# Second mixer: the four value and gate chunks projected block by block between the levels of the decayed scores

## The chip, the cores and the metric

The kernel runs on one core of a Trainium2 chip. The metric is the device time of one launch in microseconds, the median of several runs. The time before is 2326.71 us (three runs, 2320.91 to 2326.8).

## The reference, cut to what matters

A sequence of 256 tokens of width 1024 goes through two blocks. The first block has two layers, each a mixer and a mixture of 32 experts; the second has two layers with two feed-forward parts and a mixer each. The change is in the mixer of the first block's second layer, which joins a small attention (MLA) and a gated linear attention (GLA):

```
cq, ckv, krope, gq, gk, gv, gg, lr_f, lr_b = _split(x @ w_in, ODD_SPLITS)
...
k = jnp.concatenate([k_nope, jnp.broadcast_to(k_rope, ...)], -1)
mla = _merge(_blocked_attention(q, k, v, (MLA_NOPE + MLA_ROPE) ** -0.5))
...
o = _bidirectional_scan(gq_h, _heads(gk, GLA_HEADS), _heads(gv, GLA_HEADS), log_gate(lr_f, ...), log_gate(lr_b, ...))
gla = _merge(_rms_norm(o, gla_norm)) * jax.nn.silu(gg)
return jnp.concatenate([mla, gla], axis=-1) @ w_out
```

The values `gv` and the gates `gg` are 512 columns each of `x @ w_in`. The scan needs `gv` only when its scores are multiplied into values, at its very end, and `gg` after that. Nothing in `mla` needs either.

## The kernel before, in words

**Chunks.** `x @ w_in` is computed in eight chunks of 256 columns, `od(0)` to `od(7)`: 4 and 5 are `gv`, 6 and 7 are `gg`. Each weight chunk is loaded as 1 MB into one of seven ring slots (SyncE's queue). ScalarE (ACT) writes its rounded high part (`split_act`, L432, two instructions a chunk), VectorE (DVE) the rest (`split_dve`, L439, two instructions), and only then is the ring slot free for the next load. PE forms high x high + high x low + low x high (`three`), 48 matmuls of 128x256 a chunk, 24 for each of the two token blocks (`project_block_pe`, the matmuls are issued in `mm`, L228). ACT copies the bank out (`evacuate_act`, L564). There are four pairs of part buffers, so the split of chunk 6 waits until PE has used chunk 4, and so on.

**The order.** Each engine has its own queue, in program order, and waits on semaphores. `OD_ORDER` is the order of the attention for all engines, written out by hand: "scores" (PE scores; DVE maximum L771; ACT exponential L781), "gates" (the logarithms of the GLA decay: PE product, DVE L2162 and L1890, ACT Exp L1896 and Ln L1898), "probs" (DVE), "turn" (PE transposes L791), "values", "logs" (DVE L2168), "mix" (ACT copies the result). Heads 0 and 2 go first, then 1 and 3. Before the change chunk 4 is projected ahead of this order, chunks 5 and 6 inside it ("project"), and chunk 7 behind it, where the first chunk of the output weights is split too.

**The decayed scores.** `decayed_pe`, `decayed_act` and `decayed_dve` then form the scores of the scan in both directions (two streams) by halving: level 8, 7, ... 1. In a level PE multiplies `decayed` blocks (L1663 for level 8, L1673 for the others, with 64 rows of the array a head; each fp32 matmul is two records in the trace, so a stream's level is 16 records and a round of both streams 32). For each stream DVE multiplies the factors in (L1740), copies the level above through a mask (L1763, 128x256) and forms the next distance (L1724); ACT takes its exponential (L1731). DVE starts with two running sums (L1682). These functions call `aside(step)` at step 0 and once a round (steps 2 to 9); in this mixer it did nothing. The mixers of the second block use the same functions, with 128 rows a head and half as many records, and there projections do stand in `aside`.

**After it.** `decayed_values_pe` multiplies the scores by `gv` (L228, 128x128), ACT takes squares (L749), DVE and POOL the norm, the gate is multiplied in, and the output is projected (`gated_pe`, `out_pe`). The split of the output chunks releases the ring for the second experts' weights.

Of the kernel before, what the change touches and what calls it, by code (L numbers as in the profile page):

```python
# [524 lines left out]
def project_pe(e, k, key, group=A_BANKS, fresh=None):  # L525


    S = k.S
    bank = k.banks.open(e, group, key)
    if feature_major(key):  # L530
        for c in range(2):
            _, hi, lo = split_views(k, key + (c,))
            e.wait_ge(*S.low[key + (c,)])
            if fresh is not None and c == 0:
                x_ready(e, k, fresh, 1)
            mm(e, bank[:, c * T:(c + 1) * T], three([((hi[:, j, :], lo[:, j, :]), (k.xh[:, j, :], k.xl[:, j, :])) for j in range(KT)])
               ).then_inc(*S.used.tell(key + (c,)))
        return
    for tb in range(NB):
        project_block_pe(e, k, key, bank, tb, fresh)  # L540
# [1352 lines left out]
def log_sigmoid_act(e, k, tmp, key):  # L1893
# [7 lines left out]

OD_ORDER = (("scores", 0), ("scores", 2), ("project", 5), ("gates", 0), ("probs", 0), ("probs", 2), ("project", 6), ("logs", 0),
            ("turn", 0), ("turn", 2), ("gates", 1), ("values", 0), ("values", 2), ("logs", 1),
            ("scores", 1), ("scores", 3), ("probs", 1), ("probs", 3), ("turn", 1), ("turn", 3), ("values", 1), ("values", 3), ("mix", 0), ("mix", 1))
ROPES = slice(MLA_NOPE, MLA_QD)


def od(c):  # L1910
    return "od_in", 0, c
# [42 lines left out]
def od_pe(e, k, n):  # L1954
    S, b = k.S, k.od
    cos, sin, swap = (k.tab(name)[ROPES, :] for name in ("mla_cos", "mla_sin", "mla_swap"))
    project_pe(e, k, od(0), fresh=n)
    project_pe(e, k, od(1))
    project_pe(e, k, od(2), B_BANKS)
    project_pe(e, k, od(3), B_BANKS)  # L1960
    bank = k.banks.open(e, A_BANKS, ("narrow",))
    e.wait_ge(*S.dve_out[od(1)])
    for tb in range(NB):
        ins = e.transpose(bank[:, block(tb)], b.narrow[:, tb, :], k.ident)
    ins.then_inc(*S.product.tell(("narrow",)))
    view = pairs(k.banks.open(e, A_BANKS, ("cqT",))[:, :])
    e.wait_ge(*S.dve_out[od(0)])
    for j in range(2):
        for tb in range(NB):
            ins = e.transpose(view[:, j, block(tb)], b.cq[:, tb, block(j)], k.ident)  # L1970
    ins.then_inc(*S.product.tell(("cqT",)))
    bank = k.banks.open(e, A_BANKS, ("ckvT",))
    e.wait_ge(*S.dve_step["ckv"])
    for tb in range(NB):
        ins = e.transpose(bank[:, block(tb)], b.ckv[:, tb, :], k.ident)
    ins.then_inc(*S.product.tell(("ckvT",)))
    e.wait_ge(*S.wide_loaded["od"])
    for pair in range(2):
        heads = (2 * pair, 2 * pair + 1)
        bank = k.banks.open(e, A_BANKS, ("q_raw", pair))  # L1980
        e.wait_ge(*S.dve_out[("cqT",)])
        for i, h in enumerate(heads):
            ins = mm(e, bank[0:MLA_QD, i * T:(i + 1) * T], [(k.w_uq[:, j, h * MLA_QD:(h + 1) * MLA_QD], b.cqT[:, j, :]) for j in range(2)])
        ins.then_inc(*S.product.tell(("q_raw", pair)))
        bank = k.banks.open(e, A_BANKS, ("k_raw", pair))
        e.wait_ge(*S.dve_out[("ckvT",)])
        for i, h in enumerate(heads):
            ins = mm(e, bank[0:MLA_NOPE, i * T:(i + 1) * T], [(k.w_ukv[:, h * 192:h * 192 + MLA_NOPE], b.ckvT[:, 0, :])])
        ins.then_inc(*S.product.tell(("k_raw", pair)))
        bank = k.banks.open(e, A_BANKS, ("mla_v", pair))  # L1990
        for tb in range(NB):
            for i, h in enumerate(heads):
                ins = mm(e, bank[:, block(tb * 2 + i)], [(b.ckvT[:, 0, block(tb)], k.w_ukv[:, h * 192 + MLA_NOPE:(h + 1) * 192])])
        ins.then_inc(*S.product.tell(("mla_v", pair)))
    bank = k.banks.open(e, A_BANKS, ("k_rope",))
    e.wait_ge(*S.dve_out[("narrow",)])
    mm(e, bank[ROPES, 0:T], [(swap, b.narrow_T[ROPES, 0, :])]).then_inc(*S.product.tell(("k_rope",)))
    for pair in range(2):
        view = pairs(k.banks.open(e, B_BANKS, ("q_rope", pair))[ROPES, :])
        e.wait_ge(*S.act_out["q_raw", pair])  # L2000
        for i in range(2):
            ins = mm(e, view[:, i, :], [(swap, b.qh[ROPES, 2 * pair + i, :])])
        ins.then_inc(*S.product.tell(("q_rope", pair)))
    project_pe(e, k, od(4))
    out_banks = [k.banks.open(e, O_BANKS, ("mla_o", pair)) for pair in range(2)]
    for what, i in OD_ORDER:
        if what == "project":
            project_pe(e, k, od(i))
        elif what == "scores":
            view = pairs(k.banks.open(e, B_BANKS, ("mla", i))[:, :])  # L2010
            e.wait_ge(*S.dve_step["q_roped", i // 2])
            e.wait_ge(*S.act_out["k_raw", 1])
            for tb in range(NB):
                ins = mm(e, view[:, tb, :], [(b.qh[0:MLA_QD, i, block(tb)], b.kh[0:MLA_QD, i, :])])
            ins.then_inc(*S.product.tell(("mla", i)))
        elif what == "turn":
            turn_probabilities_pe(e, k, b.e1[i // 2], ("mla_pt", i), ("mla_p", i))
        elif what == "values":
            e.wait_ge(*S.act_out["mla_pt", i])
            out = out_banks[i // 2][:, (i % 2) * T:(i % 2 + 1) * T]  # L2020
            mm(e, out, [(b.v[:, kb, block(i)], b.pt[i // 2][:, kb, :]) for kb in range(NB)]).then_inc(*S.product.tell(("mla_o", i)))
        elif what == "gates":
            view = pairs(k.banks.open(e, A_BANKS, ("gate_log", i))[:, :])
            rank = slice(32 * i, 32 * i + GATE_RANK)
            for j in range(2):
                ins = mm(e, view[:, j, :], [(k.gla_w2[rank, block(j)], b.narrow_T[rank, 0, :])])
            ins.then_inc(*S.product.tell(("gate_log", i)))
    project_pe(e, k, od(7))
    decayed_pe(e, k, b.streams, lambda step: None)
    decayed_values_pe(e, k, ("gla_o",), b.streams, b.crosses, lambda side, i: 2 * i + side, b.gla_v, od(5))  # L2030
    gated_pe(e, k, "od_out", 0, ("gla_o",), ("mla_mix",))

# [7 lines left out]
def od_act(e, k):  # L2040
    S, b = k.S, k.od
# [11 lines left out]
    for pair in range(2):  # L2053
        for key, tile, r in (("q_raw", b.qh, slice(0, MLA_QD)), ("k_raw", b.kh, slice(0, MLA_NOPE))):
            e.wait_ge(*S.product[key, pair])
            evacuate_act(e, k, (key, pair), tile[r, 2 * pair:2 * pair + 2, :], pairs(k.banks[key, pair][r, :]))
    od_project_act(e, k, 4, b.gla_v[:, :, 0:256])
    for what, i in OD_ORDER:
        if what == "project":
            od_project_act(e, k, i, b.gla_v[:, :, 256:512] if i == 5 else b.gate[:, :, 0:256])  # L2060
        elif what == "scores":
            if i % 2:
                e.wait_ge(*S.product["mla_pt", i - 1])
            softmax_act(e, k, ("mla", i), b.e1[i // 2], MLA_QD ** -0.5, k.tags[:, i // 2, :])
        elif what == "turn":
            if i % 2:
                e.wait_ge(*S.product["mla_o", i - 1])
            e.wait_ge(*S.product["mla_pt", i])
            evacuate_act(e, k, ("mla_pt", i), b.pt[i // 2])
        elif what == "gates":  # L2070
            log_sigmoid_act(e, k, b.la[i], ("gate", i))
        elif what == "mix":
            if i == 0:
                e.wait_ge(*S.masks_made["all"])
            e.wait_ge(*S.product["mla_o", 2 * i + 1])
            evacuate_act(e, k, ("mla_o", i), k.mixT[:, 2 * i:2 * i + 2, :])
    od_project_act(e, k, 7, b.gate[:, :, 256:512])
    decayed_act(e, k, b.streams, lambda step: None)
    e.wait_ge(*S.act_out[od(7)])
    e.activation(b.gate, b.gate, ACT.Silu).then_inc(*S.act_out.tell(("gla_o", "gate")))  # L2080
    e.wait_ge(*S.act_out["mla_o", 1])
# [5 lines left out]
def od_dve(e, k, norm):  # L2087
# [53 lines left out]
    split_chunk(e, k, following(k, od(4)), split_dve)  # L2141
    for what, i in OD_ORDER:
        tags = k.tags[:, (i // 2) % 2, :]
        if what == "project":
            split_chunk(e, k, following(k, od(i)), split_dve)
        elif what == "scores":
            softmax_dve(e, k, ("mla", i), MLA_QD ** -0.5, tags)
        elif what == "probs":
            e.wait_ge(*S.act_out["mla", i])
# [21 lines left out]
    for i in (1, 3):  # L2171
        e.wait_ge(*S.product["mla_o", i])
    e.memset(b.diag.rearrange("p a b c -> p (a b c)"), 0.0).then_inc(*S.dve_step.tell("gla_clear"))
    split_chunk(e, k, following(k, od(7)), split_dve)
    e.wait_ge(*S.dve_step["la", 1])
    e.wait_ge(*S.act_out[od(3)])
    decayed_dve(e, k, b.streams, lambda step: None)
    mix_parts_dve(e, k, k.mixT[:, 0:4, :], (slice(0, P), slice(0, 4), slice(0, T)), ("mla_mix",))
    gated_dve(e, k, "od_out", 0, ("gla_o",), k.gla_norm[:, :], b.gate, ("gla_o", "gate"), norm)

# [765 lines left out]
```

## Time and profile before

| | |
|---|---|
| median of three runs | 2326.71 us |
| span of the profiled execution | 2323.1 us |
| what the runs' median has above that span | 3.6 us |
| TensorE (PE) busy | 2166.1 us, 93% |
| VectorE (DVE) busy | 1142.2 us, 49% |
| ScalarE (ACT) busy | 784.0 us, 34% |
| mean granted TensorE clock | 0.975 |
| HBM traffic over the span | 267 GB/s |

The profiled execution has no run time of its own beside its span, so a change in the span is taken as the same change in the median. Times in a timeline are microseconds from the start of the span. A timeline row says when a merged group of one line starts and how long it lasts; "idle before" is how long its engine had stood still and what ended that. Clock 1.00 is 2.4 GHz, 0.50 is 1.2 GHz.

### The profile page before, as it was taken

The page shows a single profiled execution, that of the slowest core. Times are in us where ns is not written, and L with a number is a line of the kernel's source. Part 1 is how long each engine was busy: PE and PEld are TensorE (multiplying, and loading weights), DVE is VectorE, ACT ScalarE, POOL GpSimd, SP SyncE. Part 2 cuts the span into 40 slices and gives each one's busy share as a digit, 9 for nine tenths or more (in the row PEclk, how much of TensorE's full clock was granted, in tenths as well). Part 3 has the DMA queues.
Part 4 walks back from the last instruction along what each step waited for, and adds up shares of the span by engine and source line. Part 5 has one row for each costly group of instructions (what it writes and reads, how often), then busy time and mean ns, then how long its engine had stood idle before and what let it go on. Part 6 is the DMA issues. An engine that isn't in the chain of part 4 may idle for free.

```text
span 2323.1 us, 30109 instructions
## 1 busy us (share of the span) xinstructions
PE 2166.1 (93%) x12126; PEld 1528.0 (66%) x12126; DVE 1142.2 (49%) x1786; ACT 784.0 (34%) x1299; POOL 61.5 (3%) x62
## 2 busy tenths in 40 slices
PE   8999998899887989997988999999999999989998
PEld 7884443443367944433433688898888788888887
DVE  5582222121156831211111666678666766787666
ACT  3441110111034321101111355454555455554553
POOL 0010000000010100000000000001000000001000
PEclk9999999899998799999999999999999999999999
DMA  9449999999972289999999864634555464534561
GB/s 289 145 175 379 421 421 421 417 421 420 413 246 73 76 363 420 420 421 415 420 420 421 295 209 168 199 128 127 181 200 200 154 208 166 193 96 159 167 208 46
DMA packets 231542, 622.66 MB, mean 268 GB/s; under 512 B 15456, under 2 KB 166944, under 8 KB 182112
## 3 DMA queue, kind: packets, MB, share of 16 engines
q1 hardware_dynamic: 226096, 605.32, 68.7%
q0 software_dynamic: 3040, 10.78, 1.5%
q10 hardware_dynamic: 2256, 4.50, 0.5%
q8 instruction: 102, 1.67, 0.3%
q14 instruction: 48, 0.39, 0.0%
HBM read 619.51 MB, written 1.05 MB: 267 GB/s over the span
## 4 chain that ended last, share of the span: by engine, by line
PE 41%; DMA 6%; DVE 4%; ACT 2%; issue 1%; POOL 0%; SPq 0%; DVEq 0%; ACTq 0%
PE bank L1517 14%; PE bank L1505 10%; PE bank L1518 7%; PE bank L228 6%; PE bank L1345 3%; DMA arena<-in_moe_w_up 1%; DMA ring<-in_moe_w_up 1%; DMA ring<-in_ffn_gate 1%; DMA w_parts<-in_moe_w_up 1%; DMA x_tok<-in_moe_w_up 1%; DVE w_low L439 1%; PE bank L1673 1%; ACT w_high L432 1%; DVE x_tok L687 0%; DVE x_tok L676 0%
## 5 line engine op out<-in xcount | busy, mean ns | idle before, releaser
L439 DVE TENSOR_TENSOR w_low<-ring,w_high 128x1024 fp32r<-128x1024 f32 x364 | 441.1, 1225 | 271.7 <-ACT w_high L432 271.7
L1517 PE MATMUL bank<-xT_parts,w_high 128*128 128x512 f32 x1408 | 496.2, 395 | 6.0 <-DVE xT_parts L504 6.0
L432 ACT ACTIVATE w_high<-ring 128x1024 fp32r<-128x1024 f32 x364 | 377.1, 1053 | 218.0 <-PE bank L1518 184.6
L1518 PE MATMUL bank<-xT_parts,w_low 128*128 128x256 f32 x1408 | 394.5, 280 | 0.0
L1345 PE MATMUL bank<-ring,arena 128*64 128x512 f32 x1344 | 339.0, 594 | 17.3 <-DMA w_parts<-in_moe_w_gate 5.3
L1517 PEld LDWEIGHTS bank<-xT_parts,w_high 128*128 128x128 f32 x1408 | 264.0, 188 | 69.0 <-DVE xT_parts L504 6.9
L1345 PE MATMUL bank<-w_parts,arena 128*64 128x512 f32 x768 | 263.8, 609 | 13.4 <-DMA w_parts<-in_moe_w_up 6.7
L1518 PEld LDWEIGHTS bank<-xT_parts,w_low 128*128 128x128 f32 x1408 | 265.8, 189 | 3.1
L1345 PEld LDWEIGHTS bank<-ring,arena 128*64 128x64 f32 x1344 | 110.1, 137 | 230.5 <-issue 221.9
L1453 DVE SCALAR_TENSOR_TENSOR arena<-arena,bank 128x512 f32<-128x512 f32 x32 | 23.9, 747 | 434.1 <-PE bank L1345 434.1
L228 PE MATMUL bank<-w_high,xT_parts 128*128 128x256 f32 x1152 | 222.9, 290 | 10.4 <-DVE w_low L439 8.8
L228 PEld LDWEIGHTS bank<-w_high,xT_parts 128*128 128x128 f32 x1152 | 186.4, 195 | 13.0 <-ACT arena L564 4.5
L228 PE MATMUL bank<-w_low,xT_parts 128*128 128x256 f32 x576 | 165.0, 286 | 0.0
L1345 PEld LDWEIGHTS bank<-w_parts,arena 128*64 128x64 f32 x768 | 81.1, 140 | 121.3 <-issue 117.0
L1468 DVE TENSOR_TENSOR arena_rounded<-bank,arena_rounded 128x512 fp32r<-128x512 f32 x64 | 41.2, 686 | 217.8 <-ACT arena_rounded L1438 217.8
L1505 PE MATMUL bank<-w_high,hidden_low 128*128 128x512 f32 x320 | 126.3, 395 | 0.0
L1505 PE MATMUL bank<-w_low,hidden_high 128*128 128x512 f32 x320 | 126.2, 394 | 0.0
L1505 PE MATMUL bank<-w_high,hidden_high 128*128 128x512 f32 x320 | 126.1, 394 | 0.0
L228 PE MATMUL bank<-xT_parts,w_high 128*128 128x256 f32 x608 | 115.7, 292 | 9.0 <-DVE xT_parts L504 6.0
L228 PEld LDWEIGHTS bank<-w_low,xT_parts 128*128 128x128 f32 x576 | 112.6, 195 | 0.2
L1438 ACT ACTIVATE arena_rounded<-bank 128x512 fp32r<-128x512 f32 x64 | 34.7, 594 | 229.0 <-PE bank L1345 229.0
L228 PEld LDWEIGHTS bank<-xT_parts,w_high 128*128 128x128 f32 x608 | 98.7, 199 | 10.8 <-issue 5.4
(284 smaller groups left out, 2934.4 us busy)
## 6 DMA issues: line engine op xcount, KB each, us to landing
ring<-in_moe_w_gate SPq DMA_DIRECT2D x56, 1024.0 KB, 24.3
ring<-in_moe_w_up SPq DMA_DIRECT2D x56, 1024.0 KB, 21.0
ring<-in_moe_w_down SPq DMA_DIRECT2D x56, 1024.0 KB, 25.8
ring<-in_ffn_gate SPq DMA_DIRECT2D x44, 1024.0 KB, 6.8
ring<-in_ffn_up SPq DMA_DIRECT2D x44, 1024.0 KB, 5.4
ring<-in_ffn_down SPq DMA_DIRECT2D x44, 1024.0 KB, 6.6
w_parts<-in_moe_w_up SPq DMA_DIRECT2D x32, 1024.0 KB, 26.1
w_parts<-in_moe_w_down SPq DMA_DIRECT2D x32, 1024.0 KB, 26.1
```

Source lines behind the costliest of these rows:

```text
L228: ins = e.matmul(out, lhs, rhs, start=first and i == 0, stop=last and i == len(parts) - 1)
L432: e.activation(hi, src, ACT.Copy).then_inc(*S.high.tell(key))
L439: e.tensor_tensor(lo, src, hi.bitcast(F32), ALU.subtract).then_inc(*S.low.tell(key))
L1345: ins = e.matmul(tile[r, :], lhs[:, half * per + kk, r], X.ring.view(chunks[j])[:, kk, BANK * n:BANK * n + BANK], start=half == 0 and kk = ...
L1438: e.activation(b.yh[:, cols], X.banks[X.key("y", g, n)][:, :], ACT.Copy).then_inc(*S.act_out.tell(X.key("y_high", g, n)))
L1453: e.scalar_tensor_tensor(out=b.silu, in0=b.silu, scalar=b.weight[:, i:i + 1], in1=X.banks[X.key("h", g)][:, :], op0=ALU.mult, op1=ALU.mult ...
L1468: e.tensor_tensor(b.yl[:, cols], X.banks[X.key("y", g, n)][:, :], b.yh[:, cols].bitcast(F32), ALU.subtract).then_inc(*S.dve_out.tell(X.key ...
L1505: ins = e.matmul(out, lhs, rhs[:, 0, cols], start=g == 0 and j == 0, stop=g == FT - 1 and j == 2)
L1517: e.matmul(pairs(bank[:, :]), hi[:, j, :], k.x_parts[:, :, j, :], start=j == 0, stop=False)
L1518: ins = e.matmul(bank[:, 0:T], lo[:, j, :], k.xh[:, j, :], start=False, stop=j == KT - 1)
L1673: ins = e.matmul(scores[:, 2 * i + blk, :], d.decayed[r, j, block(blk)], d.queries(d.decayed[r, j, block(blk)], m), start=True, stop=True)
```

## The change

Chunks 4 to 7 are taken out of the attention and put into `aside` of the decayed scores, one token block a time. ACT splits chunk 5 where it did before, chunks 6, 7 and the first output chunk in the rounds, each behind the projection that frees its buffer; DVE takes their low parts one round later.

```
-OD_ORDER = (("scores", 0), ("scores", 2), ("project", 5), ("gates", 0), ("probs", 0), ("probs", 2), ("project", 6), ("logs", 0),
+OD_ORDER = (("scores", 0), ("scores", 2), ("gates", 0), ("probs", 0), ("probs", 2), ("logs", 0),
             ("turn", 0), ("turn", 2), ("gates", 1), ("values", 0), ("values", 2), ("logs", 1),
             ...
+OD_ROUNDS = {0: (4, 0), 2: (4, 1), 3: (5, 0), 4: (5, 1), 5: (6, 0), 6: (6, 1), 7: (7, 0), 8: (7, 1)}
+OD_SPLITS = {2: ("od_in", 0, 6), 4: ("od_in", 0, 7), 6: ("od_out", 0, 0)}
...
-    project_pe(e, k, od(4))
...
-        if what == "project":
-            project_pe(e, k, od(i))
...
-    project_pe(e, k, od(7))
-    decayed_pe(e, k, b.streams, lambda step: None)
+    def beside(step):
+        if step in OD_ROUNDS:
+            c, tb = OD_ROUNDS[step]
+            bank = k.banks.open(e, A_BANKS, od(c)) if tb == 0 else k.banks[od(c)]
+            project_block_pe(e, k, od(c), bank, tb)
+    decayed_pe(e, k, b.streams, beside)
...
-    od_project_act(e, k, 4, b.gla_v[:, :, 0:256])
+    split_chunk(e, k, od(5), split_act)
...
-    od_project_act(e, k, 7, b.gate[:, :, 256:512])
-    decayed_act(e, k, b.streams, lambda step: None)
+    def beside(step):
+        if OD_ROUNDS.get(step, (0, 0))[1]:
+            c = OD_ROUNDS[step][0]
+            projected(e, k, od(c))
+            evacuate_act(e, k, od(c), (b.gla_v if c < 6 else b.gate)[:, :, 256 * (c % 2):256 * (c % 2) + 256])
+        if step in OD_SPLITS:
+            split_chunk(e, k, OD_SPLITS[step], split_act)
+    decayed_act(e, k, b.streams, beside)
...
-    split_chunk(e, k, following(k, od(7)), split_dve)
...
-    decayed_dve(e, k, b.streams, lambda step: None)
+    def beside(step):
+        if step - 1 in OD_SPLITS:
+            split_chunk(e, k, OD_SPLITS[step - 1], split_dve)
+    decayed_dve(e, k, b.streams, beside)
```

## Rows read from the trace of the kernel before

**Rows 1.** The page: span, busy time of each engine, and GB/s in 40 slices.
```profile
span 2323.1 us, 30109 instructions
...
PE 2166.1 (93%) x12126; PEld 1528.0 (66%) x12126; DVE 1142.2 (49%) x1786; ACT 784.0 (34%) x1299; POOL 61.5 (3%) x62
...
GB/s 289 145 175 379 421 421 421 417 421 420 413 246 73 76 363 420 420 421 415 420 420 421 295 209 168 199 128 127 181 200 200 154 208 166 193 96 159 167 208 46
```

**Rows 2.** The second experts: busy time by engine, granted clock, DMA share, GB/s.
```profile
830.00:1280.00 450.00, 412.38 (x2025) 183.03 (x2026) 84.13 (x146) 53.12 (x102) 0.00 (x0) 0.98 1.00 413
```

**Rows 3.** SyncE's queue, timeline of its load issues around this mixer.
```profile
704.25 35.40 SPq L358 DMA_DIRECT2D ring<-in_moe_w_gate  x4
795.74 7.85 SPq L358 DMA_DIRECT2D ring<-in_moe_w_up  x3
```

**Rows 4.** The mixer in windows: PE, PEld, DVE, ACT, POOL, clock, DMA share, GB/s.
```profile
696.90:702.80 5.90, 5.90 (x50) 5.89 (x50) 5.45 (x8) 0.00 (x0) 0.00 (x0) 1.00 0.00 0
...
702.80:717.30 14.50, 14.50 (x111) 13.73 (x110) 8.86 (x18) 10.34 (x18) 0.00 (x0) 1.00 0.44 147
...
723.00:729.70 6.70, 0.00 (x0) 0.03 (x1) 3.48 (x10) 4.53 (x11) 0.00 (x0) 0.70 0.05 20
729.70:734.70 5.00, 5.00 (x16) 3.94 (x17) 0.73 (x3) 1.79 (x3) 0.00 (x0) 0.50 0.01 3
734.70:741.30 6.60, 6.60 (x51) 6.38 (x49) 5.27 (x7) 2.49 (x3) 0.00 (x0) 0.91 0.17 29
...
750.40:781.70 31.30, 30.27 (x224) 30.09 (x224) 29.15 (x54) 11.54 (x18) 0.00 (x0) 0.50 0.00 1
781.70:787.80 6.10, 6.04 (x31) 6.07 (x32) 1.03 (x2) 2.15 (x9) 2.88 (x4) 0.56 0.16 24
```

**Rows 5.** DVE, timeline of the mixer.
```profile
705.77 0.17 DVE L773 TENSOR_SCALAR softmax_stats<-softmax_stats 128x2 f32<-128x2 f32 x1
...
711.60 0.88 DVE L2162 TENSOR_SCALAR rot_tmp<-bank,gla_b 128x256 f32<-128x256 f32 x2 [1.14 <-PE bank L228]
...
719.07 0.68 DVE L2168 SCALAR_TENSOR_TENSOR mixT<-rot_tmp,mixT 128x512 f32<-128x512 f32 x1
...
720.13 0.87 DVE L2162 TENSOR_SCALAR rot_tmp<-bank,gla_b 128x256 f32<-128x256 f32 x2
...
735.67 0.91 DVE L2173 MEMSET arena<- 128x1024 f32 x1 [5.20 <-PE bank L228]
736.93 2.36 DVE L439 TENSOR_TENSOR w_low<-ring,w_high 128x1024 fp32r<-128x1024 f32 x2 [0.35 <-ACT w_high L432]
739.21 1.22 DVE L1682 TENSOR_TENSOR_SCAN arena<-tables,mixT 128x512 f32<-128x512 f32 x1
...
745.35 0.69 DVE L1740 TENSOR_TENSOR arena<-arena 128x512 f32<-128x512 f32 x1
```

**Rows 6.** ACT, timeline of the mixer.
```profile
713.23 0.63 ACT L1896 ACTIVATE mixT<-mixT 128x512 f32<-128x512 f32 x1 [2.20 <-DVE mixT L1890]
...
715.18 0.63 ACT L1898 ACTIVATE mixT<-mixT 128x512 f32<-128x512 f32 x1
...
785.55 0.28 ACT L749 ACTIVATE acc<-bank 128x128 f32<-128x128 f32 x1 [7.28 <-PE bank L228]
```

**Rows 7.** PE, timeline of the mixer.
```profile
741.27 1.71 PE L1645 MATMUL bank<-arena 64*128 64x128 f32 x16
746.09 1.23 PE L1663 MATMUL bank<-arena 64*128 64x128 f32 x8 [3.11 <-DVE arena L1740]
748.66 1.23 PE L1663 MATMUL bank<-arena 64*128 64x128 f32 x8 [1.34 <-DVE arena L1740]
...
781.76 6.33 PE L228 MATMUL bank<-arena 128*128 128x128 f32 x32 [1.09 <-DVE arena L1763]
```

**Rows 8.** The rounds of the second block's first mixer, in one window.
```profile
1545.50:1582.00 36.50, 35.62 (x290) 34.58 (x289) 29.96 (x46) 19.16 (x31) 0.00 (x0) 1.00 0.42 129
```

**Rows 9.** PE's level matmuls (L1673) alone in that window: PE, PEld, clock, DMA share, GB/s.
```profile
1545.50:1582.00 36.50, 14.10 (x112) 13.31 (x112) 1.00 0.42 129
```

More of the change, by code:

```diff
@@ L2003, in od_pe @@
         ins.then_inc(*S.product.tell(("q_rope", pair)))
-    project_pe(e, k, od(4))
     out_banks = [k.banks.open(e, O_BANKS, ("mla_o", pair)) for pair in range(2)]
     for what, i in OD_ORDER:
-        if what == "project":
-            project_pe(e, k, od(i))
-        elif what == "scores":
+        if what == "scores":
             view = pairs(k.banks.open(e, B_BANKS, ("mla", i))[:, :])
@@ L2056, in od_act @@
             evacuate_act(e, k, (key, pair), tile[r, 2 * pair:2 * pair + 2, :], pairs(k.banks[key, pair][r, :]))
-    od_project_act(e, k, 4, b.gla_v[:, :, 0:256])
+    split_chunk(e, k, od(5), split_act)
     for what, i in OD_ORDER:
-        if what == "project":
-            od_project_act(e, k, i, b.gla_v[:, :, 256:512] if i == 5 else b.gate[:, :, 0:256])
-        elif what == "scores":
+        if what == "scores":
             if i % 2:
@@ L2143, in od_dve @@
         tags = k.tags[:, (i // 2) % 2, :]
-        if what == "project":
-            split_chunk(e, k, following(k, od(i)), split_dve)
-        elif what == "scores":
+        if what == "scores":
             softmax_dve(e, k, ("mla", i), MLA_QD ** -0.5, tags)
```

## The prediction

> **What bounds the kernel now.** First the page [rows 1]: PE is busy for 93% of the span, but the DMA traffic stands at 420 GB/s in two long stretches, which are the two mixtures of experts. So I asked next what ends a stretch of experts. In the second one the DMA share is 1.00 at 413 GB/s over 450 us while PE is busy for 412 of them [rows 2]: there the stream of weights sets the end, and it can only be started earlier. SyncE's queue shows when it starts. Four loads go out between 704 and 740, ahead of need; the next waits until 795.74, for the ring slot that the split of an output chunk frees [rows 3]. That split stands behind the whole mixer on its engine. So the mixer is a latency that goes to the end in full: a microsecond of it is a microsecond of the launch. What is asked is when the output projection and the splits beside it come.
>
> Then the mixer in windows [rows 4]. Up to 717.3 PE is busy all the time with chunks 4, 5, 6 and little attention. From 723.0 to 729.7 it does nothing: heads 1 and 3 are not ready. From 729.7 it works at clock 0.50, chunk 7 brings the clock back, and it falls again behind the idle time of 3.11 us ahead of 746.09 [rows 7]. The levels then run for 31.3 us at 0.50 throughout, with PE busy for 30.3 us and DVE for 29.2 us [rows 4]: both are nearly full, and the clock does not return although PE never rests.
>
> **What the attention loses.** On its path the gates' first addition stands at 711.60 on DVE because PE does chunk 5 first [rows 5]. Without it the product is there when DVE is through with the two maxima, at 705.9 (705.77 and 0.17). Addition and minimum take 1.6 us (711.60 on DVE to 713.23 on ACT [rows 5, 6]), Exp, table load and Ln on ACT 2.6 us (713.23 to 715.81 [rows 6]), so the logarithm is there at 710.1. The step that uses it stood at 719.07, behind the low parts of chunk 7 [rows 5]. Its 1.1 us end at 711.2, and the addition of the second gates, now at 720.13 [rows 5], comes at 711.3 if PE is ready. PE starts the transposes at 709.1, when DVE has the probabilities. These and the gate product take 2.2 us at full clock and 4.3 at half, so 711.3 or 713.3: earlier by 8.8 or 6.8 us. What hangs on it (ACT's Exp, the logarithm, the maxima of heads 1 and 3, their exponentials) keeps its spacing, and then come transposes and values, already at 0.50 in the row of 729.7 [rows 4]. At half clock the scores of head 3 may cost up to 1 us more; at full clock the last stretch is 2.5 us shorter. So 5.8 to 11.3 us; I take 7, nearer the cold end, since PE, busy in every microsecond from 696.9 to 717.3 now, will stand still for some 5 us of the 12 behind 696.9.
>
> Behind the attention DVE clears the scores (735.67, 0.91 us), takes the low parts of the first output chunk, and only then starts the sums at 739.21 [rows 5]. These low parts move into the rounds: 2.6 us less. Chunk 7 on PE (734.7 to 741.3) is not on this path; DVE's chain of sums, distances and ACT's exponential sets the first level product at 745.35 [rows 5]. It comes 9.6 us earlier, at 735.75.
>
> **What the levels gain in work.** PE now has, from there: level 8 of the two streams, which keep their distance of 2.57 us (746.09 and 748.66 [rows 7]) and are done at 740.0. Then seven token blocks. Fifty matmuls, a whole chunk among them, take 5.90 us [rows 4], a block 2.9, seven 20.3 us. The eighth (step 0) fits before level 8: PE is free from 728, DVE not until 735.75. Then seven rounds of levels. At 0.50 they cost 30.27 us for 224 records [rows 4], 4.32 a round. At 1.00 no row shows them. If they halve it is 2.2 us a round. The far bound is the second block's rate, at clock 1.00: 14.10 us for 112 records [rows 9], 0.126 each, 4.0 for 32. But there a record spans 128 rows, and here 64; at half the clock it costs 0.135 here, hardly more than there at full. Two heads on different rows must overlap, and the diagonal, the same shape, does 16 in 1.71 us at 1.00 [rows 7]. I take 2.4 us, 16.8 in all. PE ends at 740.0 + 20.3 + 16.8 = 777.1.
>
> The clock: between the block of step 0 (done about 733) and 736.5 PE idles about as long as it did ahead of 746.09, so I expect it at 0.50 again. Step 2's block then costs 2.9 us more, and the level beside it 0.6: 3.5 us, until dense work brings it back, as chunk 7 did between 734.7 and 741.3 [rows 4]. Stalls between rounds: in the second block's rounds PE idles 0.9 us of 36.5 [rows 8], with shorter levels and the same splits; I take 0.6. PE's end: 781.2, against 780.7 now.
>
> DVE beside it: from its first level product to the last copy it takes 36.2 us now, and gets three chunks of low parts of 2.36 us, 7.1 more: 735.75 + 43.3 = 779.1, or 777 without the 2.1 us that it waited in the levels. So PE sets the end, by little. ACT gets four copies of 0.6 and three splits of 2.0 to 11.5 us of work in 31: hidden, though each split waits for a projection with the next exponentials behind it. DVE waits for those, and PE has its next block meanwhile; the stalls hold this.
>
> The last copy lets the values start 1.1 us behind PE's end, at 782.3 and not 781.76 [rows 7]: 0.5 us later. The values run at 0.56 now [rows 4], 6.33 us [rows 7]; at 1.00 they are through in half of it. ACT's squares started at 785.55 [rows 6], 3.8 us behind the first value; this becomes 2.0: 1.8 us less. The table load and the silu fit before.
>
> **Sum.** At the squares the path is 0.5 - 1.8 = -1.3 us, and the rest of the mixer and the experts shift with them. The releases of the ring for gate loads two to four come later (at some 745 to 770, now by 740 [rows 3]), hidden since their tiles are not used until the experts. The span becomes 2321.8 us, and the median, which is 3.6 us over the span, 2325.4 us. In short: 9.6 us won before the levels, 10.1 lost in them, 1.8 won behind.
>
> The row that speaks loudest against the change is the clock: it falls to 0.50 where PE has stood still for 3.11 us [rows 7]. The Trainium skill says the same as a rule (TensorE: Matmul & The Clock Gate, "Why this matters for your kernels"): leave no idle gaps between bursts of matmuls, or they start at the low rate. By it the attention gives the cold end of its range, 5.8 us and not 7, and the median would be 2326.6; the trace agrees with it at 746.09. The same page (Part 3, "Packing small matmuls — row/col tiling") has small matmuls on different rows of the array run side by side. By it the levels halve to 2.2 us a round, and the sum would be 1.4 us lower.
>
> **Rivals.** *Slower: the clock does not come back in the rounds.* For it speaks that it stayed at 0.50 for 31.3 us of levels without a pause [rows 4], and half of a round is still levels. Against it, the second block's rounds, with projections in them, hold 1.00 for 36.5 us [rows 8], and chunk 7 restored it. Each further round at 0.50 costs 2.9 + 1.9 = 4.8 us; two of them give +8.3, so it decides from there: 2335. All seven, with the values cold too, give about +31. *Levels at the far rate* of 4.0 us: +11.2 - 1.3 = +9.9, 2336.6. Both together 0.16.
>
> *Faster: DVE sets the end.* If the clock holds before level 8 and the levels halve, PE ends at 740.0 + 20.3 + 15.1 = 775.4 and DVE's 777 decides; values start at 778, 4 us earlier, -5.8 with their own gain, and with a warm attention -10.1: 2316.6. For it: DVE's share in the rounds is as high as PE's. Against it: the idle stretches. All of it 0.17.
>
> *The earlier end is hidden.* If the stream of experts started by something else, nothing moves: 2326.7. Against it, no load is issued between 740 and 795.74 [rows 3]. Chance 0.07.
>
> **The numbers.** 0.3% (7 us) is about what a measurement of this kernel can tell from no change. My own case has 0.60 and its own range is 2320 to 2331. With the hidden case it makes 0.67 for the same, 0.17 faster, 0.16 slower. The range for 8 in 10 reaches into both sides: 2317 to 2335.
>
> **What would show it.** Right: PE idle in the attention and clock 0.50 there; the sums (L1682) at about 729.6; clock 1.00 from the second round on; rounds of 5.3 to 5.7 us with PE full; values at 782 and 3 us long. Wrong: clock 0.50 in the rounds, levels over 3 us a round, DVE waiting for ACT's exponentials with PE idle, or PE's idle time ahead of level 8 closed by the block.

## The result, and the profile after

The changed kernel takes 2331.11 us (median of 9 runs, 2326.68 to 2332.96), the kernel before in the same series 2323.87 (9 runs, 2320.78 to 2326.8). The ratio is 1.0027, 95% interval 1.0018 to 1.0035: slower by 6.3 us by the ratio, and by 7.2 between the two medians. The forecast was no change that can be told, with 1.3 us less. The profiled execution took 2331.11 us for a span of 2329.0, so 2.1 us lie around a span; the 3.6 us of the prediction held some of the spread between runs.

The page of the changed kernel, lines as in [rows 1]:

```profile
span 2329.0 us, 30109 instructions
...
PE 2164.7 (93%) x12126; PEld 1526.2 (66%) x12126; DVE 1142.6 (49%) x1786; ACT 783.2 (34%) x1299; POOL 61.5 (3%) x62
...
GB/s 294 148 195 364 420 421 421 418 420 420 404 231 37 85 347 420 420 421 416 421 420 421 324 183 196 190 134 114 182 213 191 156 212 166 190 100 154 172 206 48
```

The work is the same to the instruction. SyncE's queue shows the stream of the second experts start 6.9 us later than in [rows 3]:

```profile
702.90 74.33 SPq L358 DMA_DIRECT2D ring<-in_moe_w_gate  x4
802.62 7.86 SPq L358 DMA_DIRECT2D ring<-in_moe_w_up  x3
```

The spans differ by 5.9 us, so most of what the mixer loses reaches the end, as read from [rows 2].

The mixer in windows (columns as in [rows 4]):

```profile
697.60:714.70 17.10, 13.53 (x33) 9.11 (x34) 12.27 (x24) 8.56 (x16) 0.00 (x0) 0.50 0.19 62
...
733.60:745.40 11.80, 7.03 (x40) 6.41 (x40) 7.07 (x11) 4.15 (x8) 0.00 (x0) 0.71 0.00 0
745.40:755.50 10.10, 10.04 (x57) 9.73 (x57) 5.14 (x9) 3.04 (x7) 0.00 (x0) 0.50 0.32 105
755.50:787.30 31.80, 31.72 (x313) 30.41 (x312) 26.35 (x44) 12.07 (x17) 0.00 (x0) 1.00 0.20 67
789.10:792.40 3.30, 3.24 (x17) 3.27 (x18) 0.85 (x1) 0.00 (x0) 2.39 (x3) 0.60 0.01 1
```

The first part of the attention ran at 0.50. Then come 11.8 us with PE idle for 4.8 of them, 10.1 us at 0.50, and only from 755.5 on rounds at 1.00 with PE full. DVE's timeline (its counterparts are in [rows 5]):

```profile
725.97 0.91 DVE L2182 MEMSET arena<- 128x1024 f32 x1 [4.40 <-PE bank L228]
726.80 1.16 DVE L1682 TENSOR_TENSOR_SCAN arena<-tables,mixT 128x512 f32<-128x512 f32 x1
...
732.90 0.68 DVE L1740 TENSOR_TENSOR arena<-arena 128x512 f32<-128x512 f32 x1
...
748.42 0.69 DVE L1740 TENSOR_TENSOR arena<-arena 128x512 f32<-128x512 f32 x1 [1.93 <-PE bank L1673]
...
757.24 0.69 DVE L1740 TENSOR_TENSOR arena<-arena 128x512 f32<-128x512 f32 x1 [4.70 <-PE bank L1673]
```

The first level product starts at 732.90 and not 745.35: the gain in front is there. PE's timeline (against [rows 7]):

```profile
733.63 0.72 PE L1663 MATMUL bank<-arena 64*128 64x128 f32 x8 [3.32 <-DVE arena L1740]
...
745.46 4.68 PE L1673 MATMUL bank<-arena 64*128 64x64 f32 x32 [2.94 <-ACT arena L1772]
755.49 2.65 PE L1673 MATMUL bank<-arena 64*128 64x64 f32 x32
...
784.67 2.61 PE L1673 MATMUL bank<-arena 64*128 64x64 f32 x32
789.16 5.44 PE L228 MATMUL bank<-arena 128*128 128x128 f32 x32 [1.88 <-DVE arena L1763]
```

Level 7 waits 2.94 us for L1772. That is ACT's copy of the level-8 (cross) scores out of their banks, and level 7 needs the banks. ACT's timeline (against [rows 6]) shows what stood ahead of it:

```profile
742.56 0.60 ACT L564 ACTIVATE arena<-bank 128x512 f32<-128x512 f32 x1 [5.01 <-PE bank L228]
743.05 1.99 ACT L432 ACTIVATE w_high<-ring 128x1024 fp32r<-128x1024 f32 x2
744.94 0.65 ACT L1772 ACTIVATE arena<-bank 128x256 f32<-128x256 f32 x2
...
792.43 0.28 ACT L749 ACTIVATE acc<-bank 128x128 f32<-128x128 f32 x1 [3.74 <-PE bank L228]
```

ACT stood still for 5.01 us until PE had finished block 1 of chunk 4, copied it, split chunk 6, and only then copied the cross scores, ready since about 737. PE waited for ACT, which had waited for PE.

### The profile page after: what moved, and what is told of

Same layout as the page of the kernel before. It is cut to its first block, busy times and chain, and to the rows that moved or that the text cites. A ratio compares the mean times of both kernels' runs of the same rounds, so it can differ in the third digit from the quotient of the medians.

```text
span 2329.0 us, 30109 instructions
## 1 busy us (share of the span) xinstructions
PE 2164.7 (93%) x12126; PEld 1526.2 (66%) x12126; DVE 1142.6 (49%) x1786; ACT 783.2 (34%) x1299; POOL 61.5 (3%) x62
## 4 chain that ended last, share of the span: by engine, by line
PE 41%; DMA 6%; DVE 4%; ACT 2%; issue 1%; POOL 0%; SPq 0%; DVEq 0%; ACTq 0%
PE bank L1517 14%; PE bank L1505 10%; PE bank L1518 7%; PE bank L228 6%; PE bank L1345 3%; DMA arena<-in_moe_w_up 1%; DMA ring<-in_moe_w_up 1%; DMA ring<-in_ffn_gate 1%; DMA w_parts<-in_moe_w_up 1%; DMA x_tok<-in_moe_w_up 1%; DVE w_low L439 1%; PE bank L1673 1%; ACT w_high L432 1%; DVE x_tok L687 0%; DVE x_tok L676 0%
## 5 line engine op out<-in xcount | busy, mean ns | idle before, releaser
L1505 PE MATMUL bank<-w_high,hidden_low 128*128 128x512 f32 x320 | 126.3, 395 | 0.0
```

The source lines that it names most:

```text
L1505: ins = e.matmul(out, lhs, rhs[:, 0, cols], start=g == 0 and j == 0, stop=g == FT - 1 and j == 2)
```

## The experiments

Theory A: this order on ACT's queue is the loss, by its wait and by the clock behind it. Theory B: there is more PE work in the rounds than they hide, in any order. Theory C: the pauses decide the clock, and it the rounds. Executions start this mixer some microseconds apart, so the table counts from ACT's first copy of `x` in it (652.23 before, 650.88 after): start of the sums (L1682), of the first level product (L1740), end of the last masked copy (L1763), start of the first square (L749). Ratios are to the kernel before on the same chip.

| kernel | sums | level product | last copy | square | ratio (95% interval) |
|---|---|---|---|---|---|
| before | 87.0 | 93.1 | 129.3 | 133.3 | 1 |
| changed | 75.9 | 82.0 | 138.0 | 141.6 | 1.0027 (1.0018 to 1.0035) |
| e1_cross_first | 75.7 | 81.8 | 130.8 | 134.3 | 1.0008 (0.9997 to 1.0020) |
| e2_cross_first_warm | 75.7 | 81.8 | 132.8 | 135.1 | 1.0005 (0.9995 to 1.0015) |
| e3_chunk4_in_front | 75.4 | 81.5 | 132.8 | 135.2 | 1.0003 (0.9994 to 1.0012) |
| e4_thin_blocks | 75.7 | 81.8 | 129.2 | 133.4 | 1.0006 (0.9996 to 1.0016) |
| e5_both | 75.6 | 81.7 | 130.5 | 133.7 | 1.0006 (0.9996 to 1.0016) |
| e6_idle_filled | 75.3 | 81.4 | 126.3 | 130.3 | 0.9988 (0.9979 to 0.9997) |
| e7_idle_filled_warm | 74.8 | 80.9 | 125.7 | 130.1 | 0.9990 (0.9981 to 1.0000) |
| e8_cross_first_warm_values | 75.8 | 81.9 | 130.9 | 133.1 | 0.9998 (0.9989 to 1.0007) |
| e9_idle_filled_warm_levels | 74.7 | 80.8 | 122.2 | 124.3 | 0.9967 (0.9957 to 0.9976) |
| e10_before_warm_levels | 87.0 | 93.1 | 128.8 | 131.0 | 0.9989 (0.9981 to 0.9998) |

**e1_cross_first.** In `decayed_act`, for this mixer:

```
-            if m == 7:
+            if m == 7 and not early:
                 decayed_cross_act(e, k, d)
...
+        for d in streams if m == 8 and early else []:
+            decayed_cross_act(e, k, d)
         aside(n + 2)
```

> The changed kernel, but ACT copies the level-8 (cross) scores out of their banks before it waits for block 1 of chunk 4, not behind that copy and the split of chunk 6. Theory A (the queue order on ACT): the 2.94 us that PE waits for that copy ahead of level 7 go, and the clock, which fell to 0.50 behind them for a round, holds or returns earlier; 3 to 7 us less than the changed kernel, a ratio to the kernel before of 0.9997 to 1.0015. Theory B (there is more PE work in the rounds than they hide, whatever the order): only the wait itself goes, up to 3 us, and the rounds keep their length; 1.0015 to 1.0027. Theory C (the idle time ahead of level 8 decides the clock): the wait goes, the round after it stays at 0.50; 1.0013 to 1.0018.

The wait ahead of level 7 is gone and the clock holds in the rounds. Two stretches, level 8 with block 1 of chunk 4 and level 7, and the rounds behind:

```profile
734.80:746.80 12.00, 9.40 (x73) 8.78 (x73) 7.37 (x12) 5.42 (x11) 0.00 (x0) 0.72 0.00 0
746.80:782.20 35.40, 35.27 (x337) 33.75 (x336) 31.79 (x54) 14.48 (x22) 0.00 (x0) 1.00 0.27 90
```

The square comes 7.3 us earlier than in the changed kernel: 2.9 us of wait and 4.4 of clock, which did not fall behind it. By the ratios it is 4.4 us, and their intervals overlap narrowly (1.0018 to 1.0020), so the gain of the whole launch is not clear of the noise by itself. Theory A holds for most of the loss. e8, with the same rounds, held the clock too. The kernel before is not beaten, though: what is won in front (11.3 us) is still lost in the rounds (PE 35.27 of 35.40 us busy), as B says of the rest.

**e2_cross_first_warm.** Ahead of level 8, behind the block of step 0:

```
+            for _ in range(7 if step == 0 else 0):
+                e.matmul(bank[:, 256:512], k.ident, k.busy_columns[:, 0:256], start=True, stop=True)
```

> As e1_cross_first, and in addition seven idle matmuls (identity by 256 columns, into the half of chunk 4's bank that is written next) between the block of step 0 and level 8, where PE stood still for 3.32 us. They add work and no result. Theory C: the clock stays at 1.00 from the attention's end through the rounds, block 1 of chunk 4 takes 3.1 and not 5.15 us, and the launch is 3 to 5 us shorter than e1. Theories A and B: the clock ahead of level 7 matters little once the copy is early, 0 to 2 us.

Block 1 of chunk 4 took 3.12 us and not 5.15, as C says. But nothing is won, because the clock now fell three times in the rounds. Stretches ahead of such a fall and behind it (windows, the two times):

```profile
742.30:745.70 3.40, 3.40 (x37) 3.19 (x35) 3.37 (x7) 1.04 (x2) 0.00 (x0) 1.00 0.82 294
745.70:749.10 3.40, 3.40 (x17) 3.28 (x17) 3.33 (x8) 0.22 (x1) 0.00 (x0) 0.50 0.00 0
755.90:759.30 3.40, 3.40 (x36) 3.19 (x35) 3.37 (x7) 1.26 (x2) 0.00 (x0) 1.00 0.66 265
759.30:762.80 3.50, 3.50 (x19) 3.50 (x18) 3.09 (x7) 0.00 (x0) 0.00 (x0) 0.51 0.00 0
```

PE never stood still ahead of the falls. Of the 37 records of the first stretch 32 are level matmuls of 64x64. So the clock can fall without a pause. But not every such stretch is followed by a fall: in e1 the same work as in the first row, the level matmuls of the same round, kept 1.00, and so did all that came behind it up to the values:

```profile
749.80:753.20 3.40, 3.40 (x36) 3.21 (x35) 3.37 (x7) 1.26 (x2) 0.00 (x0) 1.00 0.71 282
```

What made the difference between e1 and e2 is not shown.

**e3_chunk4_in_front.** Chunk 4 back where it was, steps 0 and 2 empty:

```
-OD_ROUNDS = {0: (4, 0), 2: (4, 1), 3: (5, 0), ...
+OD_ROUNDS = {3: (5, 0), ...
...
+    project_pe(e, k, od(4))
     out_banks = ...
...
-    split_chunk(e, k, od(5), split_act)
+    od_project_act(e, k, 4, b.gla_v[:, :, 0:256])
```

> The changed kernel with one part undone: chunk 4 is projected in front of the attention as in the kernel before, where DVE still turns the queries; steps 0 and 2 of the rounds hold no block, the other six blocks stay. Theory B: a block of chunk 4 is free in front (scores of head 0 are not used before DVE is through with the low parts of chunk 5) and costs 5.15 us in the rounds, so some 5 us less than the changed kernel, ratio 1.0005 or lower. Theory A: the same copy waits only for the split of chunk 6 now, no longer for a block; the wait of PE shrinks to under 1 us and the gain is 5 to 9 us, ratio 0.9988 to 1.0005. If the clock in the attention is what matters the attention is shorter too, by up to 2 us.

The square is 6.4 us earlier than in the changed kernel, the sums only 0.5: the projection in front is free. But two blocks fewer do not make the rounds short, since PE still waited 2.42 us for the cross copy, where theory A expected under 1 us: ACT does the split of chunk 6 first (1.99 us). The clock stood at 0.50 from 732.4 to 749.5.

**e4_thin_blocks.** Three of the 24 matmuls in each block. The kernel leaves out seven of the eight row tiles that values and gates are formed from, so its result is not that of the reference.

> The changed kernel with 3 of the 24 matmuls in each block of chunks 4 to 7, so the values and gates are formed from one of eight row tiles: all waits and copies stand, the work of the blocks is almost gone. Theory B: the rounds fall to DVE's length, 4.1 us each and 6.5 with low parts, about 36 to 43 us from the first level product to the last copy instead of 56; the launch is 12 to 18 us shorter than the changed kernel, and the attention shows its gain of 11 us undisturbed. Theory A: most of the loss is in waits that remain, and it is 2 to 8 us shorter. With so little dense work the clock may stay at 0.50 in all rounds, as in the kernel before, which then still gives 4.3 us of levels a round.

This is the miss that says most, for theory B. With almost no block work the last copy comes 8.8 us earlier than in the changed kernel, where B expected 12 to 18 for the launch, and 1.6 us earlier than in e1. From the first level product to the last copy it takes 47.4 us and not 36 to 43. The last sentence of the expectation, that the clock may stay at 0.50, came true. The rounds, one window:

```profile
743.00:781.20 38.20, 38.16 (x242) 35.92 (x242) 32.33 (x54) 16.43 (x25) 0.00 (x0) 0.50 0.25 83
```

PE is full again, at 0.50: a round takes 5.6 us, 4.7 of levels and the rest block, against 5.6 to 6.2 in e1 with whole blocks at 1.00 (2.6 and 3.1, and up to 0.7 more where DVE takes low parts). The wait of 2.94 us ahead of level 7 is still in this kernel and not in e1. Theory B in its plain form falls. Most of what a thin block saves is lost to the clock: 0.3 us a round remains.

**e5_both.** e1 and e3 together.

> The cross copies first (e1) and chunk 4 in front (e3) together: six blocks in the rounds and no wait of PE for ACT ahead of level 7. If the work of a block is what is left of the loss, the two add up: 5 us less than e1 at the end of the rounds, ratio to the kernel before about 0.9985. If the clock rules (e3's clock stood at 0.50 for 17 us from level 8 on, since nothing dense was left there), the rounds start cold without the dense block of chunk 4 and the gain over e1 is under 2 us, ratio 1.0000 to 1.0008.

They do not add up: the square is at 133.7 against 134.3 in e1. PE waits only 0.52 us for the cross copy now, but the clock was at 0.50 from 733.4 to 747.1, where the dense block of chunk 4 is missing. The second of its two expectations holds.

**e6_idle_filled.** The blocks go where PE stood still:

```
+OD_ORDER = (("scores", 0), ("scores", 2), ("gates", 0), ("block", 0), ("probs", 0), ("probs", 2), ("logs", 0),
+            ("turn", 0), ("turn", 2), ("gates", 1), ("high", 6), ("values", 0), ("values", 2), ("logs", 1),
+            ("scores", 1), ("scores", 3), ("block", 1), ("probs", 1), ("probs", 3), ("evacuate", 5), ("low", 6),
+            ("turn", 1), ("turn", 3), ("values", 1), ("values", 3), ("mix", 0), ("mix", 1))
+OD_ROUNDS = {0: ((6, 0), (6, 1)), 4: ((7, 0),), 6: ((7, 1),)}
+OD_COPIES = {2: 6, 7: 7}
+OD_SPLITS = {0: ("od_in", 0, 7), 2: ("od_out", 0, 0)}
+OD_LOWS = {2: ("od_in", 0, 7), 4: ("od_out", 0, 0)}
```

The lines that carry these steps out are left out here. "block" is a block of chunk 5, "high" and "low" are the splits of chunk 6 on ACT and DVE, `OD_COPIES` are ACT's copies, `OD_LOWS` DVE's low parts by step. Chunk 4 is in front, the cross copies first.

> Blocks only where PE stood still in the changed kernel's profile: chunk 4 in front of the attention, the blocks of chunk 5 behind the gate product and behind the scores of heads 1 and 3, both blocks of chunk 6 ahead of level 8 (6.4 us idle from the end of the values on), only chunk 7 in the rounds (steps 4 and 6); chunk 6's low parts in DVE's idle time behind the probabilities, cross copies first. Theory B (a round costs what its block costs, 3.1 us, against DVE's 4.1 us a round without one): two blocks instead of seven or eight, levels done 6 to 9 us earlier than e1, ratio 0.9965 to 0.9980. If the clock falls in rounds without a block, the levels take 36 us as before and the end is 9 to 11 us of attention gain ahead of the kernel before, less two blocks: ratio 0.9970 to 0.9985. Both ways faster than the kernel before; wrong if over 0.9990.

Faster than the kernel before: the sums stay at 75.3, so four blocks (chunks 5 and 6) and a split fitted into the attention and behind it at no cost, and the square is 3.0 us earlier. The gain is smaller than either range of the expectation (0.9965 to 0.9980, 0.9970 to 0.9985). The levels did not end 6 us earlier than e1's, only 4.5 us at the last copy; they ran partly at 0.50, and e9 tests whether that is why. One window from level 8 to the end:

```profile
736.90:781.40 44.50, 37.61 (x289) 35.90 (x289) 37.84 (x65) 16.14 (x26) 0.00 (x0) 0.68 0.15 48
```

**e7_idle_filled_warm** and **e8_cross_first_warm_values.** In `decayed_values_pe`, added to e6 and to e1:

```
+        for _ in range(4 if tb == 0 and key == ("gla_o",) else 0):
+            e.matmul(bank[:, 0:256], k.ident, k.busy_columns[:, 0:256], start=True, stop=True)
```

> As e6_idle_filled, with four idle matmuls ahead of the values, where PE waits 1.9 us for DVE's last masked copies and the clock fell to 0.50 for the first values. If that fall costs, 1 to 2 us less than e6; if the squares hang on DVE or the clock is down anyway, the same as e6 within 0.5 us.

> As e1_cross_first, with the four idle matmuls ahead of the values. The prediction had the values at 1.00 and 1.8 us cheaper; in the changed kernel and in e1 they ran at 0.50. If it is the pause of 1.9 us that lowers the clock, the first value to ACT's first square takes 2.0 and not 3.2 us, and the launch is 1 to 2 us shorter than e1, ratio about 1.0002.

In e8 the first square comes 2.2 us behind the last copy (783.82 against 781.65) and 3.5 in e1, and is 1.2 us earlier; the clock stayed at 1.00. So the prediction's 1.8 us for the values are real where PE is not left waiting. In e7 the clock was down already: the idle matmuls ran at 0.50, took 3.54 us and held the first value back to 2.5 us behind the last copy. The values then ran at 1.00 (3.73 us and not 6.40), and the square was as in e6.

**e9_idle_filled_warm_levels.** e7 with idle matmuls in the levels:

```
+def idle_pe(e, k, count):
+    e.wait_ge(*k.S.act_out["mla_o", 1])
+    for _ in range(count):
+        e.matmul(k.banks["mla_o", 1][:, 0:256], k.ident, k.busy_columns[:, 0:256], start=True, stop=True)
...
+    if m == 8 and d.key == ("gla", 1):
+        idle_pe(e, k, 4)
...
+        idle_pe(e, k, {2: 5, 3: 3, 5: 3, 7: 3, 8: 3}.get(step, 0))
```

> As e7_idle_filled_warm, with idle matmuls (identity by 256 columns into a bank that is free) between the two streams' level 8 (4), behind it (5) and in four of the rounds that hold no block (3 each). In e6 and e7 the levels without a block ran at 0.50 for 17 and 10 to 14 us. If the clock is what the lighter rounds lose, the levels run at 1.00 all along and DVE sets them: first level product to last copy 39 to 41 us instead of 44.9, the launch 3 to 5 us shorter than e7, ratio 0.9970 to 0.9980. If DVE's low parts and copies set them at either clock, the same as e7 within 1 us.

This beats both kernels: 2315.66 us (12 runs, 2313.24 to 2322.41) against 2325.25, ratio 0.9967. The levels in one window, and the square:

```profile
732.20:770.90 38.70, 38.18 (x331) 33.68 (x331) 35.66 (x61) 15.96 (x26) 0.00 (x0) 0.96 0.17 55
```

```profile
774.98 0.28 ACT L749 ACTIVATE acc<-bank 128x128 f32<-128x128 f32 x1 [5.37 <-PE bank L228]
```

At clock 0.96 the first product to the last copy takes 41.4 us against 44.9 in e6, though PE has more to do; that is 3.5 of the 5.8 us by which the square is earlier than in e7. The other 2.3 come at the values, whose idle matmuls now take 1.99 us and not 3.54. DVE is busy for 35.7 of 38.7 us, and part of PE's 38.2 us are idle matmuls: with the clock held, DVE is the next limit, or close to it.

**e10_before_warm_levels.** The kernel before, with the same idle matmuls (6 at step 0, 5 at step 2, 3 in the others, 4 ahead of level 8's second stream and of the values).

> The kernel before, nothing moved, with idle matmuls ahead of level 8 (6), between its streams (4), behind it (5), in each round (3) and ahead of the values (4). What the clock alone is worth there. DVE was busy for 29.2 of 31.3 us of its levels, so at most 2 us there, and 1.5 to 2 us in the values at 1.00: ratio 0.9984 to 0.9990, and the 0.50 stretch of 41 us gone. If the move of the blocks brings something beyond the clock, e9 must lie clearly below this one.

```profile
746.00:782.00 36.00, 35.72 (x306) 30.34 (x305) 33.92 (x62) 13.83 (x22) 0.00 (x0) 1.00 0.01 2
```

1.00 throughout, the levels 0.5 us shorter, the square 2.3 us earlier, ratio 0.9989. The clock alone is worth that where DVE (33.9 of 36.0 us) sets the levels. e9 lies clearly below, so the moved blocks and the earlier cross copies together are worth some 5 us beside it.

## Why the prediction was wrong, point by point

The way was wrong: 8.2 us later at the first square (141.6 against 133.3), where 1.3 us earlier were forecast. By its own steps:

- **The attention.** Right, and undersized. The sums start 11.1 us earlier (9.6 forecast), mostly at 0.50 as taken. All kernels with this order of gates show 11.1 to 12.3.
- **ACT in the rounds: the step that failed.** "ACT gets four copies of 0.6 and three splits of 2.0 to 11.5 us of work in 31: hidden, though each split waits for a projection with the next exponentials behind it. DVE waits for those, and PE has its next block meanwhile". Behind the first split stood not only exponentials but the cross copies, and these hold the banks of level 7, which stands ahead of PE's next block in its queue. PE waited 2.94 us, and e1, which moves only these copies, does not have the wait. I had asked what waits on DVE behind a late ACT, and not who waits for each copy. PE's timeline of the kernel before already named it, for 0.52 us at level 7:

```profile
750.41 30.27 PE L1673 MATMUL bank<-arena 64*128 64x64 f32 x224 [0.52 <-ACT arena L1772]
```

- **The clock in the rounds.** The fall at level 8 was forecast and came (0.50 from 735.1 on; block 1 of chunk 4 took 5.15 us). It returned, as forecast, but fell again behind the wait, at 745.4, until 755.6. Level 7 and its block took 10.0 us and not the 5.6 of a warm round: 4.4 us, or 4.1 more than the 5.9 that the sum has for them (5.3, and 0.6 for a cold level). e1 shows both prices together, 7.3 us.
- **A warm round.** 5.3 us and stalls of 0.6 over all were taken; five rounds from 755.49 to 784.67 took 5.84 each. Levels 2.6 (2.4 taken, 2.2 had they halved), up to 3.25 in two rounds with DVE's low parts, blocks 3.1 (2.9 taken): terms of the sum set too low, 2.7 us in these five rounds, or 2.1 beyond the stalls taken. Wait, cold round and warm rounds (2.9 + 4.1 + 2.1), less 0.7 for block 1, which took 5.15 us and not 5.8, and 0.5 for level 8 and the last level give the 8.9 us by which PE's levels lasted longer than forecast (53.65 us from level 8 to the end against 44.7).
- **The values.** "At 1.00 they are through in half of it" did not happen: PE waited 1.88 us for the last masked copies, the clock fell at 789.7, and the square came 3.3 us behind the first value and not 2.0, after a wait 0.8 us longer than forecast. e8 shows the forecast size where the pause is filled.
- **The rivals.** The slower one named the right resource (the clock) but not the cause: it asked whether blocks hold it. In the rounds behind 755.5, in e1 and in e8 they do, and what the changed kernel has ahead of its fall in the rounds is a wait. But e2 shows that the clock can fall beside blocks too, without a wait. "Hidden" is refuted: the loads of the experts moved with the mixer. "DVE sets the end" is nearest in e9 and e10, where the clock was held by idle matmuls.

That adds up: 8.9 + 0.8 + 1.3 for the levels and values, less 1.5 for the attention, is 9.5 us from -1.3 to 8.2. The row "loudest against the change", the clock, was a fair warning and priced too low.

What stays open: why the clock falls in the rounds of e2 and not in those of e1 and e8 is not settled, so 4.4 us is what the fall cost in this execution, not a fixed price of such a wait; each profile is a single execution. The times of e1 to e5 can't be told from one another, nor those and e8 from the kernel before; their order rests on the profiles alone. The gains of e6 and e7 are small against the spread (their intervals end at 0.9997 and 1.0000); e9's is clear.

## What to carry to other kernels

Work moved beside a loop is paid for at its place in every queue: for each instruction put ahead of another ask who waits for that one, down to copies that only free a bank. Before removing work that PE does in an idle stretch or a light loop, check what it does for the clock: here a round with thin blocks at 0.50 took 5.6 us, and 5.6 to 6.2 with full ones at 1.00. First fill the places where PE waits for others; only what is left belongs into a loop whose other engine is nearly full.

## What was not expected of the hardware

The clock fell to 0.50 with PE never idle, behind stretches of almost only 64x64 level matmuls (e2, 32 of 37 records between 742.3 and 745.7), while in e1 it stayed at 1.00 through the same ones. And a level round at 1.00 takes 2.6 us for 32 records, 0.081 us each, against 0.146 at 0.50 (4.68 us in the changed kernel): a record of 64 rows costs less than one of the second block's on 128 rows (0.126 at 1.00), as the prediction took from heads on different rows overlapping.
